# The gate's first columns computed inside the delta rule's inverse instead of inside the RWKV inverse

## What is computed

```
h    = rms_norm(x)
cols = split(h @ w_in)
y_gdn  = gated delta rule (6 heads, both directions, chunks of 128 tokens)
y_mla  = softmax attention over low rank keys and values (6 heads)
y_rwkv = RWKV-7 recurrence (4 heads, both directions)
mix  = concat(y_gdn, y_mla, y_rwkv) * silu(cols['gate'])
x    = x + mix @ w_out
```

## Time and profile before

| what | us |
|---|---|
| median of 3 runs | 1341.04 |
| lowest and highest of them | 1337.54 and 1343.74 |
| the profiled execution's own time | 1339.64 |
| its span in the trace | 1337.8 |

### The profile page before, as it was taken

How to read it: one execution, slowest core, us unless ns; L and a number is a source line. 1 busy time by engine, 2 the same in 40 slices (tenths; PEclk the granted TensorE clock), 3 DMA queues, 4 the chain that set the end, 5 groups by cost and what they waited for, 6 DMA issues and landing times. The chain is left out here.

```text
span 1337.8 us, 17866 instructions
## 1 busy us (share of the span) xinstructions
PE 1280.6 (96%) x7013; PEld 923.3 (69%) x7013; DVE 745.5 (56%) x1425; ACT 345.1 (26%) x745; POOL 51.8 (4%) x92
## 2 busy tenths in 40 slices
PE   6999999999999999999999899999899999998997
PEld 5887549994448675699844487658577686576783
DVE  2144466675350123666744448964885369666872
ACT  2243412120011134121100322144441231325422
POOL 1100000000000000000000000100300000202000
PEclk9999999999999999999999999999999999999999
DMA  8732106454443331354454342230010631110000
GB/s 265 244 113 91 63 15 214 151 189 181 155 167 126 126 126 64 126 170 149 187 188 164 134 145 93 74 116 2 1 48 1 207 139 63 64 64 1 1 2 32
DMA packets 65978, 149.21 MB, mean 112 GB/s; under 512 B 2225, under 2 KB 8263, under 8 KB 65895
## 3 DMA queue, kind: packets, MB, share of 16 engines
q1 hardware_dynamic: 62320, 141.47, 30.0%
q0 software_dynamic: 1216, 3.52, 1.0%
q10 hardware_dynamic: 2359, 3.07, 0.8%
HBM read 146.96 MB, written 1.07 MB: 111 GB/s over the span
## 5 line engine op out<-in xcount | busy, mean ns | idle before, releaser
L1323 ACT ACTIVATE region<-banks 128x384 f32<-128x384 f32 (+8 forms) x154 | 74.4, 483 | 328.7 <-PE banks L430 119.9
L430 PE MATMUL banks<-hnT,weight_slabs 128*128 128x256 f32 x608 | 137.4, 387 | 4.3 <-DVE hnT L1795 4.3
L430 PEld LDWEIGHTS banks<-hnT,weight_slabs 128*128 128x128 f32 x608 | 117.3, 194 | 23.2 <-DVE hnT L1795 5.4
L482 PE MATMUL banks<-weight_slabs,region 128*128 128x512 f32 x256 | 115.1, 592 | 0.0
L1936 DVE TENSOR_TENSOR region<-banks,region 128x128 f32<-128x128 f32 x40 | 11.7, 292 | 144.9 <-PE banks L595 144.0
L482 PEld LDWEIGHTS banks<-weight_slabs,region 128*128 128x128 f32 x256 | 48.5, 190 | 60.3 <-issue 60.3
L482 PE MATMUL banks<-region 128*128 128x512 f32 x192 | 87.6, 592 | 0.0
L1778 DVE TENSOR_TENSOR region<-region 128x256 f32<-128x256 f32 (+23 forms) x160 | 75.7, 473 | 17.5 <-ACT region L1665 12.1
L1778 DVE TENSOR_TENSOR region<-weight_slabs 128x1024 f32<-128x1024 f32 x32 | 39.2, 1225 | 80.6 <-PE banks L482 76.4
L1778 DVE TENSOR_TENSOR region<-weight_slabs,region 128x1024 f32<-128x1024 f32 x64 | 78.2, 1221 | 1.1
L1279 POOL TENSOR_TENSOR region<-region,consts 128x240 f32<-128x240 f32 (+24 forms) x60 | 34.4, 599 | 993.5 <-DVEq L1787 972.7
(11 more groups left out here) (355 smaller groups left out, 2141.1 us busy)
## 6 DMA issues: line engine op xcount, KB each, us to landing
weight_slabs<-in_mlp_w SPq DMA_DIRECT2D x32, 2048.0 KB, 8.6
weight_slabs<-in_w_in SPq DMA_DIRECT2D x10, 2048.0 KB, 7.8
weight_slabs<-in_od_w_in SPq DMA_DIRECT2D x6, 2048.0 KB, 7.9
weight_slabs<-in_ev_w_in SPq DMA_DIRECT2D x5, 2048.0 KB, 11.9
weight_slabs<-in_w_out SPq DMA_DIRECT2D x4, 2048.0 KB, 8.1
weight_slabs<-in_ev_w_out SPq DMA_DIRECT2D x2, 2048.0 KB, 8.3
weight_slabs<-in_od_w_out SPq DMA_DIRECT2D x2, 2048.0 KB, 8.0
weight_slabs<-in_w_in SPq DMA_DIRECT2D x2, 2016.0 KB, 7.5
```

The costliest lines, as they stand in the source:

```text
L430: ins = mm(view(ps, b + i * S, (1, S)), view(slabs, o + k * width + c0, (1, P)), view(hnT, k * S, (1, S)), start=k == 0, stop=k == KC - 1)
L482: ins = mm(view(ps, b, (1, 512)), view(R, act + k * st, (1, P)), view(w, wt + k * step_, (1, 512)), start=n == 0 and k == 0, stop=n == 7 a ...
L1323: say(A(dst, view(ps, b, *(dims or ((1, n),)), np_=np_), ACT.Copy, scale=scale), read("scalar", *key))
```

## The change

Gate piece 0 of tile 0 leaves the RWKV inverse; there one constant matmul each stands at ("Y", 1), ("Z", 1) and ("Z", 2), in the ring "short". Both tiles of piece 0 are computed in the delta rule's inverse, one after the other in bank 5, with sixteen places in `GATES`; the eight constant matmuls there are gone. ScalarE's tanh of tile 0 moves behind its copy of the second transposed probabilities in ("Z", 0) of the delta rule's inverse, and VectorE's `gate_mul(0, 0)` from base step 6 to ("Z", 0), behind `rwkv_variance`.

```
 TensorE, RWKV inverse
@@ fill_inverse
                     elif (what, n) in (("Y", 0), ("Z", 0)):
                         fill(2)
-                    elif what not in ("Yhalf", "Zhalf"):
-                        for _ in range(2):
-                            next(first_gate, None)
-                first_gate = late_gate(L, 0, "long")
+                    elif what in ("Y", "Z"):
+                        warm(1)
                 invert(("r", L), "r", fill_inverse)
...
                         for _ in filler:
-                            pass
-                        for _ in first_gate:
                             pass
 TensorE, delta rule's inverse
@@
-                gate_steps = late_gate(L, 1, "hold")
+
+                def gate_products():
+
+                    for t in range(T):
+                        yield from late_gate(L, t, "hold")
+                        yield
+                gate_steps = gate_products()
@@
-                GATES = {("base", 14): 3, ("Yhalf", 0): 2, ("Zhalf", 0): 1, ("Yhalf", 1): 1, ("Zhalf", 1): 1}
-                WARM = (("base", -1), ("base", 14), ("Z", 0), ("Y", 1), ("Z", 1), ("VT", 2), ("Z", 2), ("X", 2))
+                GATES = {("base", 8): 1, ("base", 10): 1, ("base", 14): 3, ("Yhalf", 0): 2, ("Z", 0): 1,
+                         ("Y", 1): 2, ("Yhalf", 1): 2, ("Z", 1): 2, ("Zhalf", 1): 1, ("VT", 2): 1}
@@ mla_between
-                    if (what, n) in WARM:
-                        warm(1, "five")
                     for _ in range(GATES.get((what, n), 0)):
                         next(gate_steps, None)
 ScalarE
@@
                 say(A(view(hn, QN + 576 + 64, (672, 2), (1, 32)), ...), up("uprojected", L))
-                gate_tanh(0, 0)
@@ mla_between, ("Z", 0)
                         mla_exp(3)
                         copy_out(view(hn, MPT(1), (1, 512)), "mPT", L, 1)
+                        gate_tanh(0, 0)
 VectorE
@@ gdn_between
                         if n == 2:
                             rope()
-                        if n == 6:
-                            gate_mul(0, 0)
@@
                     if (what, n) == ("Z", 0):
                         mla_max(3)
                         rwkv_variance()
+                        gate_mul(0, 0)
```

## The result

The changed kernel takes 1364.91 us (median of 4 runs, 1364.17 to 1366.4) against 1342.2 us for the kernel before in the same comparison: a ratio of 1.0179, with a 95% interval of 1.0154 to 1.0205. It is 1.8% slower. The forecast was 1346.3 us with a range of 1336 to 1352.

A forecast was written before the change was run, and what follows sets the result against it. TensorE, busy 96% of the span, bounds the delta inverse's chain, while VectorE's waits cap the RWKV gain. Per layer -1.7 + 3.7 = +2.0, two layers +4.0, with clock +5.3, on 1341.04: 1346.3 us, range 1336 to 1352.

The forecast's parts named there:

- part 3, the clock: TensorE's clock behind the thinned inverses: one fall to 0.50 in the two layers, +1.3 us, bounds 0 and 5.2 us.
- the fall at 906: Existing fall behind layer 2's RWKV inverse: a group of twelve records takes 2.92 us instead of 1.60, priced at 1.3 us.
- Rival 3: The clock falls behind the delta inverse and in the RWKV inverse's last levels, 1.3 us each: 1350.2 us, chance 0.25.
- one of two layers: At 954 to 956 the clock is 0.50, at layer 3's like place 1.00, so it falls in one layer of two.
- RWKV inverse, -1.7 us per layer: Eight gate matmuls out, three constant ones in; only VectorE's waits of 0.86 and 0.85 us are won, bounds 0.9 and 4.3.
- Delta inverse, +3.7 us per layer: Sixteen filling matmuls stay sixteen but stand where the chain runs, `gate_mul` in VectorE's run: +3.7 us, bounds 0 and 5.2.
- the 1.3 us of Y: Delta inverse, level 0: VectorE's early blocks end at 968.24, Y starts near 968.35, +1.3 us, VectorE's following run moving with it.
- The steps for ("Yhalf", 1) and ("Z", 1): Delta inverse, level 1: one more matmul at each, 0.86 us each, both arriving, from 2.0 to 2.9 to 3.7 us.
- Places that "give back nothing": Delta inverse: the matmuls removed from ("base", -1), ("Z", 2) and ("X", 2) stood in idle time, so removal changes 0 us.
- Rival 1: The delta inverse is neutral, sixteen matmuls for sixteen; only 2 x -1.7 = -3.4 us remains: 1337.6 us, chance 0.22.
- rival 2: TensorE is the bound in both inverses, so all ten matmuls fewer count, 8.6 us: 1332.4 us, chance 0.08.
- +2.0 was forecast: Sum per layer without the clock: -1.7 us in the RWKV inverse and +3.7 us in the delta inverse.

The follow-up runs named there:

- experiment 1: The changed kernel with the two constant matmuls back at ("Z", 2) and ("X", 2) of the delta inverse: 1350.89 us, 1.0069 of the kernel before.
- experiment 2: The kernel before without its two constant matmuls at ("Z", 2) and ("X", 2) of the delta inverse: 1356.82 us, ratio 1.0116.
- experiment 3: The changed kernel with only the constant matmul at ("X", 2) of the delta inverse back: 1349.37 us, 1.0061 of the kernel before.
- experiment 6: The changed kernel with two constant matmuls behind the first products after the delta inverse, in both layers: 1360.41 us, 1.0152 of the kernel before.
- experiment 4: The kernel before with only the RWKV inverse thinned, leaving out seven of eight matmuls of gate piece 0, tile 0: 1340.77 us, ratio 0.9994.
- experiment 7: The kernel before with gate tile 0's eight matmuls placed in waits of both inverses and its tanh ahead of the rope wait: 1334.52 us, ratio 0.996.

## Why the prediction was wrong

**The step that failed is part 3, the clock.** It was put as "I take one fall in the two layers, +1.3", with an upper bound of "4 x 1.3 = 5.2 us". The place was named rightly, the end of the delta inverse, and so was the cause, the two constant matmuls at ("Z", 2) and ("X", 2). Of the waits that they leave, the step had only the last, "1.2 us or more" (1.35 us); the 0.99 us in front of Z's second half were not in it. The number of falls was too low, two of two instead of one of two, and above all the size was: stretch E lost 8.03 us in each layer, six times the 1.3 us, so that the term is 16.1 us at this place alone where the sum had 1.3. The price was taken from the fall at 906, which lasts 3.4 us, with a group of 128 columns (L939) right in it. Behind the delta inverse come 8 us of products of 64 columns, at full rate, before the first group of 128 (1002.01 to 1010.2). Experiments 1, 2 and 3 showed that the fall is the whole of stretch E's loss, and experiment 6 that what is put behind the wait sets its length. Rival 3 was the right rival with a chance of 0.25 and a price of 9.2 us where the two profiles differ by 24.8 us. The section "A second HAM failure mode: psum-queue depth-cycling" of the Trainium skill's page "TensorE: Matmul & The Clock Gate", which stood beside it, tells of another case (bf16, 512 columns). It says which way the clock goes, and the traces agree with its direction: 0.50 for 17.1 us behind waits of 0.99 and 1.35 us. It gave no size for this place, and I weighed it at a quarter.

One reading behind the "one of two layers" was off: the rope's fall at 954 to 956 has its like in layer 3 at 1237 to 1239, 283 us later, and not at 1234 to 1236. The granted clock is 1.00 there too, so the step does not change.

Point by point:

- *RWKV inverse, -1.7 us per layer.* As a matter of the queue it is right: stretch A is 1.86 us shorter. VectorE's waits went as the steps said, and TensorE now waits 1.10 us for ScalarE and 0.88 us for VectorE's decay steps:

```profile
900.09 2.22 PE L1005 MATMUL banks<-region 128*128 128x64 f32 x16 [1.10 <-ACT region L1550]
903.19 2.93 PE L939 MATMUL banks<-consts,hn 128*128 128x128 f32 x12 [0.88 <-DVEq L1787]
```

  But the clock falls behind idle time there, for 6.8 us instead of 3.4 us. Stretch B gave back 2.42 and 1.19 us, and experiment 4 shows the part alone to be worth nothing. "I take 1.7" left out that thinning brings falls of its own; only the third rival had them. Where no fall comes, as in layer 2 of experiment 7, stretch A is 22.55 us and B 24.88 us, and the whole 1.86 us are kept.
- *Delta inverse, +3.7 us per layer.* Stretches C and D together are 4.58 and 4.65 us longer, falls of the clock in C included. From the heads' first transpose to the first product after the inverse it was to be 48.6 us and is 1006.78 - 957.75 = 49.03 us. The rows that decide it, of the changed kernel:

```profile
957.75 0.42 PE L419 MATMUL banks<-consts,hn 128*96 128x128 f32 x2 [0.76 <-ACTq L1695]
...
969.01 1.48 PE L800 MATMUL banks<-region 128*128 128x16 f32 x12 [0.32 <-issue]
...
973.91 1.76 DVE L2167 TENSOR_TENSOR region<-region,consts 128x1536 f32<-128x1536 f32 x1
...
979.97 0.69 DVE L2314 SCALAR_TENSOR_TENSOR region<-region,banks 128x512 f32<-128x512 f32 x1 [0.15 <-DVE small L2498]
...
980.80 1.96 PE L889 MATMUL banks<-weight_slabs,hnT 128*128 128x512 f32 x4 [0.63 <-DVE region L2314]
...
983.30 1.50 PE L800 MATMUL banks<-region 128*128 128x32 f32 x12 [0.54 <-issue]
```

  `gate_mul` stands directly behind the variance, ScalarE's tanh was early enough, and TensorE waits 0.63 us for bank 5, as the step said. The missing 0.4 us: VectorE's level matrix moved by 973.91 - 971.57 - 0.61 = 1.7 us against the heads, not by the 1.3 us of Y. It was not released by Y: VectorE runs to it without a gap from its last base read, which moved by 965.26 - 962.93 - 0.61 = 1.7 us. The steps for ("Yhalf", 1) and ("Z", 1) gave 1.7 us: from 983.30 to 1006.78 it is 23.48 us, and it was 1002.01 - 980.24 = 21.77 us.
- *Places that "give back nothing"*: ("Z", 2) and ("X", 2) gave back nothing to the queue, as written, and cost 8 us each layer through the clock. Costing an edit at nothing because the engine waits there was right for the queue and wrong for the kernel.
- *Rival 1 and rival 2* are out: the delta inverse was not neutral, and the five matmuls fewer per layer shortened stretch A by 1.86 us, not by 4.3 us.

The queue's part alone can be put together from places without a fall: -1.86 us in stretch A, 24.66 - 23.31 = +1.35 us in stretch C (layer 3 of experiment 1 and of the kernel before) and +2.81 us in stretch D, that is +2.3 us per layer where +2.0 was forecast. The rest, some 20 us, I put down to the clock: 16.1 us in stretch E, 3.6 us in stretch B, 0.8 us in stretch C. For stretch E the experiments show it. For B and C it is what is left over; all kernels without a fall there have the same B, 24.8 to 24.9 us, whether the inverse is thinned or not. Which layer a fall in stretches A to C lands in changed from kernel to kernel, and what decides it is open.

## What to carry to other kernels

Before taking a filling matmul out of a wait, look at the granted clock of what comes behind it and at the form of those products: the price of a fall is not the usual length of a fall but up to half of the time that it lasts, and that depended on what followed: 17.1 us where products of 64 columns came next for 14 us, 6.8 us with two matmuls of 512 columns among them, 3.4 us at 906 with a group of 128 columns directly behind. A wait of 1 to 3 us of TensorE between small products is a place to put work into, useful or not: here three constant matmuls per layer made the kernel 0.55% faster (0.36 to 0.73%), 4.9 us of it seen in the stretches that they touch. And price the clock at its worst when its cover is what the change removes; a fall seen elsewhere in the trace gives a price for that place only.

## What the runs showed of the hardware that was not expected

- With TensorE and its weight loads busy throughout (16.00 and 15.77 of 16 us), the granted clock stayed at 0.50 for 17.1 us, in four of four such places (the changed kernel and experiment 2, both layers). The first 14 us of it are products of 64 columns; it came back within the groups of 128 columns behind them. The same products ran at 1.00 throughout in eighteen of eighteen places where a constant matmul stood at ("X", 2). So in these runs they neither raised the clock nor let it fall.
- The difference between the two was one float32 matmul of 512 columns, 0.86 us, ahead of a wait (experiment 3). The idle time in front of the products became 0.30 us instead of 1.35 us, with 1.00 us of idle time shortly before it in both cases.
- Falls in the second block lasted 3.4, 6.8, 10.2 or 17.1 us, and two matmuls of 512 columns behind the wait cut the 17.1 us to 6.8 us (experiment 6).
